# First stage of a two-block transformer kernel: two modulation blocks change engines, transfers are reordered, idle products are added on TensorE

## The reference

```python
c_act = jax.nn.silu(c)
mod = (c_act @ w_ada[l] + b_ada[l])[:, None, :]          # 1024 -> 6 * 1024
sh_m, sc_m, ga_m, sh_f, sc_f, ga_f = jnp.split(mod, 6, axis=-1)
h = _rms_norm(x, g_pre_mix[l]) * (1.0 + sc_m) + sh_m
y = _hybrid_mixer(h, ...)                                 # begins with h @ w_in
```

## Time and profile before

| what | value |
|---|---|
| median of 3 runs | 2115.19 us (2115.07 to 2115.41) |
| the profiled execution's own time | 2114.72 us |
| its span | 2112.9 us |
| TensorE busy | 2070.6 us, 98% |
| VectorE busy | 1385.5 us, 66% |
| ScalarE busy | 530.4 us, 25% |
| GpSimd busy | 806.1 us, 38% |
| VectorE's memsets of `ones` and `eps` (L480, L481) end | 0.99 us |
| VectorE's diagonal blocks of the norm (L493) end | 17.25 us |
| first product of the first half (L1029) | 26.64 us |
| first product of the second half (L1049) | 46.32 us |

### The profile page before, as it was taken

How to read it: one execution, slowest core, us unless ns; L and a number is a source line. 1 busy time by engine, 2 the same in 40 slices (tenths; PEclk the granted TensorE clock), 3 DMA queues, 4 the chain that set the end, 5 groups by cost and what they waited for, 6 DMA issues and landing times. The chain is left out here.

```text
span 2112.9 us, 25818 instructions
## 1 busy us (share of the span) xinstructions
PE 2070.6 (98%) x9793; PEld 1663.5 (79%) x9793; DVE 1385.5 (66%) x2297; ACT 530.4 (25%) x1256; POOL 806.1 (38%) x595
## 2 busy tenths in 40 slices
PE   8999999999999999999999999999999999999998
PEld 4446777777788888888888888888656888888887
DVE  7987956655343885376588886664626468888545
ACT  3443433333431000001401111113243431111101
POOL 0100200000104666656178887630011127787742
PEclk9999999999999999999999999999999999999999
DMA  9752555545322444453222323431132123232331
GB/s 379 242 185 76 157 182 178 156 129 143 113 80 80 160 160 160 135 168 110 86 80 80 120 68 106 126 120 50 43 123 80 50 92 99 80 113 62 82 84 40
DMA packets 244557, 252.27 MB, mean 119 GB/s; under 512 B 10010, under 2 KB 194772, under 8 KB 244180
## 3 DMA queue, kind: packets, MB, share of 16 engines
q1 hardware_dynamic: 243552, 249.17, 37.0%
q10 hardware_dynamic: 884, 1.46, 0.3%
HBM read 245.12 MB, written 4.21 MB: 118 GB/s over the span
## 5 line engine op out<-in xcount | busy, mean ns | idle before, releaser
L2809 POOL TENSOR_TENSOR w_sums<-ring 128x512 f32<-128x512 f32 x34 | 47.5, 1396 | 372.2 <-POOLq L1647 291.8
L2070 PE MATMUL ps<-h_act,ring 128*128 128x256 f32 x512 | 112.9, 379 | 0.9 <-PEq L1647 0.6
L2856 POOL TENSOR_TENSOR hidden<-rstd,h_act 128x256 f32<-128x256 f32 x34 | 32.2, 947 | 204.7 <-DVE h_act L3161 204.7
L2070 PEld LDWEIGHTS ps<-h_act,ring 128*128 128x128 f32 x512 | 96.8, 190 | 14.4 <-issue 1.5
L1049 PE MATMUL ps<-h_act,ring 128*128 128x512 f32 (+1 forms) x240 | 104.2, 593 | 0.0
L3161 DVE TENSOR_TENSOR h_act<-ps,rstd 128x256 f32<-128x256 f32 x46 | 19.5, 423 | 126.3 <-PE ps L2776 91.8
L2543 POOL TENSOR_TENSOR w_sums<-ring 128x256 f32<-128x256 f32 x96 | 89.8, 963 | 12.9 <-PE ps L2322 12.9
L2322 PE MATMUL ps<-pair_args,ring 128*128 128x256 f32 x384 | 90.7, 379 | 0.0
L2822 POOL TENSOR_TENSOR w_sums<-ring 128x768 f32<-128x768 f32 (+1 forms) x24 | 41.4, 1724 | 125.9 <-DMA ring<-in_ffn_w_out 84.0
L837 PE MATMUL ps<-h_act,ring 128*128 128x256 f32 x352 | 88.6, 394 | 0.7 <-ACT x_res L888 0.6
L849 PE MATMUL ps<-h_act,ring 128*128 128x256 f32 x352 | 88.5, 387 | 0.5 <-ACT rstd L896 0.5
(11 more groups left out here) (596 smaller groups left out, 5183.3 us busy)
## 6 DMA issues: line engine op xcount, KB each, us to landing
ring<-in_ffn_w_in SPq DMA_DIRECT2D x66, 1024.0 KB, 7.5
ring<-in_w_gate_up SPq DMA_DIRECT2D x22, 1024.0 KB, 7.8
ring<-in_ffn_w_out SPq DMA_DIRECT2D x32, 704.0 KB, 6.5
mod_half<-in_w_ada SPq DMA_DIRECT2D x16, 1024.0 KB, 8.7
ring<-in_w_mod SPq DMA_DIRECT2D x8, 2048.0 KB, 8.0
ring<-in_w_in SPq DMA_DIRECT2D x7, 2048.0 KB, 9.9
ring<-in_ffn_w_out SPq DMA_DIRECT2D x8, 1408.0 KB, 6.8
ring<-in_w_down SPq DMA_DIRECT2D x16, 704.0 KB, 6.6
```

The lines of the kernel that those rows point to most:

```text
L2070: ins = pe.matmul(K.ps[O.banks[i]][:, 0:b - a], w[:, k, (d % 4) * P:(d % 4) * P + P], K.h[:, k, CTX + a:CTX + b], start=(k == O.first(i)), ...
L2809: pool.tensor_tensor(s1, a21, a22, ALU.add).then_inc(S["wsum"].sem, 1)
L2856: pool.tensor_tensor(one[:, j], F.gate1[u % 2], F.got21[u % 2], ALU.mult)
```

## The change

Four things are done together.

1. Twenty-four idle products of 128 columns (`keep_running`, operands all ones, result unused) stand ahead of everything on TensorE; one and two more, of 512 columns, stand around `row_columns`.
2. Block 0 is now split: VectorE does k = 0 to 5 (`shift_sums`, six steps), TensorE k = 6 and 7 as a row. Block 2 is a row on TensorE, its first half of four products as soon as the first half of the transfer has landed; the spreading of the norm (`across`) stands in the middle of it. `shift_columns` adds the two parts of block 0: eight one-column products, four over 128 partitions, four over one.
3. SyncE's order: only half of the `dq` weights (k = 0 to 3) is loaded early, then the half blocks of blocks 1 and 3, then the context, then the rest of `dq`, then the constants.
4. The context is transposed two pieces at a time, two pairs between the last products of the first half and two behind it, and the waits for the context copies, the constants and the last normalised pieces stand further back on TensorE. On VectorE the normalising of k = 4 to 7 moves behind `half_sums`.

The semaphore `gates_in` becomes `parts_in` with counts that are 16 higher, and two counts in later stages follow; nothing else changes there.

```diff
+    def shift_sums():
+        w = K.ring.take(dve, ("ada", 0)).rearrange("p (k n) -> p k n", k=KT)
+        K.mods_summed += 2
+        acc = K.sq[:, 0, :]
+        for k in range(SHIFT_BY_DVE):          # 6
...
     dve.wait_ge(S.silu_done, 1)
-    sums_behind_row()
+    shift_sums()
     dve.wait_ge(S.across, 2)
...
-    for k in range(4, KT):
-        normalised(k)
     half_sums(2)
     half_sums(3)
+    for k in (4, 5):
+        normalised(k)
     coefficients(1)
+    for k in (6, 7):
+        normalised(k)
...
     act.wait_ge(S.across, 1)
-    act.activation(S.row, K.ps[7][0:1, :], ACT.Copy).then_inc(K.mod_sum, 1)
+    act.activation(S.row_shift, K.ps[1][0:1, :], ACT.Copy).then_inc(S.silu_done, 1)
+    act.wait_ge(S.across, 3)
+    act.activation(S.row, K.ps[0][0:1, :], ACT.Copy).then_inc(K.mod_sum, 2)
     start_scaled(K, S, act, 0)
...
 def start_tensor(K, S, pe):
+    pe.wait_ge(S.set_done, 1)
+    keep_running(K, pe, K.ps[7][:, 0:P], K.ones[:, :], 24)
     pe.wait_ge(S.ident_in, 16)
...
-    first_row(K, S, pe)
...
+    pe.wait_ge(S.par_done, 3)
+    first_rows(K, S, pe)
+    shift_columns(K, S, pe)
+    pe.wait_ge(S.kept, KT)
+    keep_running(K, pe, K.ps[1][:, :], K.x[:, 0, CTX:TOK], 1)
     row_columns(K, S, pe)
-    first_columns(K, pe, 2)
-    pe.wait_ge(S.par_done, 3)
-    pe.wait_ge(S.kept, KT)
+    keep_running(K, pe, K.ps[1][:, :], K.x[:, 0, CTX:TOK], 2)
...
+def first_rows(K, S, pe):
     w = K.ring.take(pe, ("ada", 0)).rearrange("p (k n) -> p k n", k=KT)
     pe.wait_ge(S.silu_done, 1)
+    for k in range(SHIFT_BY_DVE, KT):
+        last = pe.matmul(K.ps[1][0:1, :], K.cc1[:, k:k + 1], w[:, k, :], start=(k == SHIFT_BY_DVE), stop=(k == KT - 1))
+    last.then_inc(S.across, 1)
+    w = K.ring.take_begun(pe, ("ada", 2)).rearrange("p (k n) -> p k n", k=KT)
     for k in range(KT):
+        if k == 4:
+            across(K, S, pe)
+            K.ring.take(pe, ("ada", 2))
+        last = pe.matmul(K.ps[0][0:1, :], K.cc1[:, k:k + 1], w[:, k, :], start=(k == 0), stop=(k == KT - 1))
     last.then_inc(S.across, 1)
+def keep_running(K, pe, bank, rhs, n):
+    for _ in range(n):
+        pe.matmul(bank, K.ones[:, :], rhs, start=True, stop=True)
+def shift_columns(K, S, pe):
+    pe.wait_ge(K.dve.sem, SHIFT_BY_DVE)
+    pe.wait_ge(S.silu_done, 2)
+    for c in range(4):
+        pe.matmul(K.ps[7][:, c:c + 1], K.sq[:, 0, c * P:c * P + P], K.ones[:, 0:1], start=True, stop=False)
+        last = pe.matmul(K.ps[7][:, c:c + 1], S.row_shift[:, c * P:c * P + P], K.ones[0:1, 0:1], start=False, stop=True)
+    last.then_inc(K.mod_mm, 1)
...
-                    if (j, k) == (3, 2):
+                    if j == 3 and k in (1, 2):
+                        start_context(K, S, pe, k - 1)
+                    if (j, k) == (3, 3):
                         first_columns(K, pe, 3)
...
-            pe.wait_ge(S.ctx_kept, KT)
-            pe.wait_ge(S.const_in, 16)
-            pe.wait_ge(S.normed, KT)
+            start_context(K, S, pe, 2)
+            start_context(K, S, pe, 3)
```

More of the change, by code:

```diff
@@ L107 @@
 MODS_START = 4
+SHIFT_BY_DVE = 6
 MODS_FIRST = 6
@@ L283, in load_ahead @@
             name, parts = self.items[i]
-            for j, (dst, src) in enumerate(parts):
+            for j, (dst, src) in enumerate(parts[0:1] if name == "dq" else parts):
                 landed = self.begun[name] if j == 0 and name in self.begun else self.filled[i % RING]
@@ L554, in start_scalar, with context_turned @@
     act.wait_ge(S.across, 1)
-    act.activation(S.row, K.ps[7][0:1, :], ACT.Copy).then_inc(K.mod_sum, 1)
+    act.activation(S.row_shift, K.ps[1][0:1, :], ACT.Copy).then_inc(S.silu_done, 1)
+    act.wait_ge(S.across, 3)
+    act.activation(S.row, K.ps[0][0:1, :], ACT.Copy).then_inc(K.mod_sum, 2)
     start_scaled(K, S, act, 0)
-    for k in range(KT):
-        act.wait_ge(S.turned, KT + k + 1)
-        act.activation(K.x[:, k, 0:CTX], S.ctx_bank(k), ACT.Copy).then_inc(S.ctx_kept, 1)
+    context_turned(K, S, act, range(2))
+def context_turned(K, S, act, pairs):
+    for p in pairs:
+        act.wait_ge(S.turned, KT + p + 1)
+        act.activation(K.x[:, 2 * p:2 * p + 2, 0:CTX], S.ctx_bank(p).rearrange("p (a b) -> p a b", a=2),
+                       ACT.Copy).then_inc(S.ctx_kept, 1)
 def start_scaled(K, S, act, half):
@@ L589, in start_tensor, with start_context @@
         pe.transpose(K.ps[g - 1][:, 0:n], S.prow[0:n, g, :], const(K, "ident")[0:n, 0:n]).then_inc(S.par_t, 1)
-    first_row(K, S, pe)
[L591 to L595, removed]
-    row_columns(K, S, pe)
-    first_columns(K, pe, 2)
-    pe.wait_ge(S.par_done, 3)
-    pe.wait_ge(S.kept, KT)
-def start_context(K, S, pe, k):
-    if k == 0:
+    pe.wait_ge(S.par_done, 3)
[3 more added lines that the diff above has]
+    keep_running(K, pe, K.ps[1][:, :], K.x[:, 0, CTX:TOK], 1)
+    row_columns(K, S, pe)
+    keep_running(K, pe, K.ps[1][:, :], K.x[:, 0, CTX:TOK], 2)
+def start_context(K, S, pe, p):
+    if p == 0:
         pe.wait_ge(S.x_in[2], 16 * CC)
[L606 to L609, removed]
+    if p >= 2:
+        pe.wait_ge(S.ctx_kept, p - 1)
+    for i, (k, t) in enumerate(itertools.product((2 * p, 2 * p + 1), range(CC))):
+        last = pe.transpose(S.ctx_bank(p)[:, i * P:i * P + P], S.cr[t][:, k * P:k * P + P], const(K, "ident"))
     last.then_inc(S.turned, 1)
@@ L627, in start_sync @@
         sp.dma_start(S.half_buf[i][:, :, :], ada[:, 4 * half:4 * half + 4, 512 * n:512 * n + 512]).then_inc(S.half_in[i], 16)
+    for t in range(CC):
+        sp.dma_start(S.cr[t], c[:, t, :]).then_inc(S.x_in[2], 16)
+    K.ring.load_rest(sp, "dq")
     sp.dma_start(K.cst[:, P:NCONST], A["consts"][:, P:NCONST]).then_inc(S.const_in, 16)
@@ L1019, in _ @@
             start_tensor(K, S, pe)
-            w = K.ring.take(pe, "dq")
+            w = K.ring.take_begun(pe, "dq")
             for j in range(4):
```

79 lines of the change are left out of this document (39 added, 40 removed).

## The result

| kernel | median | runs | ratio to before |
|---|---|---|---|
| before | 2114.59 us (2112.20 to 2115.41) | 8 | |
| changed | 2120.52 us (2118.29 to 2121.34) | 8 | 1.0029 (1.0020 to 1.0038) |

The change costs 5.9 us. That is more than the 0.2% (4.2 us) that I had called no change, and above my range (up to 2119.8). The profiled execution took 2120.18 us with a span of 2118.4.

The account below looks back on a forecast made before the run. TensorE, busy 98% of the span, bounds the kernel. Block 2's row, added parts, idle products and columns put the first half at 31.1; plus 17.3, T moves +2.0: 2115.19 + 2.0, rounded to 2117.2 us, range 2114.8 to 2119.8.

Parts of the forecast that it names:

- first half: TensorE's stretch of products up to T: forecast to begin at 31.1 and take 17.3 us if the clock holds.
- adding block 0's parts: Eight one-column products of `shift_columns` on TensorE behind block 2's row, at 0.24 each: 1.94 us from 25.6.
- two idle products, wait for h: Between `row_columns` and the first half on TensorE: two idle products, 0.86 each, 1.72 us, where the wait took 1.40 before.
- T: Start of the second half's first product on TensorE: 46.32 before, forecast 48.3; its shift was to be the end's.
- The sum with the clock held: Main case: TensorE's clock does not fall ahead of T; T +2.0, time 2117.2 us, chance 0.57.
- first rival: Idle products don't hold the clock ahead of the first half: 1.7 us, T +3.7, 2118.9; 0.22 together with the second rival.
- A credit that never came: 2.4 us lost before between 26.64 and T, mostly to half clock; the forecast had this stretch without a gap.
- Behind T: After the second half's start: VectorE loses about 2.5 us, TensorE 2.0; VectorE has room, so nothing gained or lost.
- The second rival: Clock falls while TensorE waits for block 0 and parameters, 13.2 to 15.6: T +3.2, 2118.4; 0.22 together with first rival.
- The third rival: Clock falls both near 15 and between 25 and 31: +4.9, 2120.1; 0.10, including a fall together with a wait.
- The fourth: Rival: added work does not lie on the chain; T +0 or -0.3, time 2114.9 to 2115.2, chance 0.08.
- Faster by more than 0.2%: Whole kernel over 4.2 us faster: no mechanism, since the loss between 26.64 and T is 2.4 us; chance 0.03.

Follow-up runs that it names:

- a_again: The changed kernel profiled once more, unaltered, to see its clock; one execution, 2120.47 us.
- b_cols: b_order with eight more one-column products, results unused, ahead of `row_columns`; 2117.25 us, ratio 1.0013 to before.
- a_no_late: The changed kernel without its three idle products of 512 columns around `row_columns`; 2118.55 us, ratio 1.0019 to before.
- b_order: The kernel before with the change's transfer order, context pairs, VectorE order and later waits, but the old block division and no idle products; 2114.05 us, ratio 0.9999.
- b_early: The kernel before with only the 24 idle products at the start added; 2114.70 us, ratio 1.0004 to before.
- a_no_early: The changed kernel without the 24 idle products at the start; 2120.89 us, ratio 1.0032 to before.
- a_row: a_no_late with VectorE's part of block 0 summed by one row product in the middle of block 2's row; 2116.70 us, ratio 1.0013 to before.
- best1: b_order with the 24 idle products at the start and the filled gap of b_fill; 2112.36 us, ratio 0.9992 to before.
- b_order_fill: b_order with the filled gap of b_fill, without the 24 early idle products; 2112.27 us, ratio 0.9990 to before; repeated, 2111.92 us, 0.9989.
- b_fill: The kernel before with one 512-column and two 128-column idle products in the 1.40 us gap ahead of the first half; 2115.21 us, ratio 1.0004.
- a_mid: a_no_late with the eight one-column products of `shift_columns` moved to the middle of block 2's row; 2119.47 us, ratio 1.0023 to before.

## Why the prediction was wrong

The direction and the chain were right, the size was not. By its own steps, each against the profile after:

| step | forecast | measured | off by |
|---|---|---|---|
| block 2's row ends | 25.60 | 25.77 | +0.2 |
| adding block 0's parts | 1.94 | 2.48 | +0.5 |
| one idle product | 0.86 | 1.60 | +0.7 |
| `row_columns` | 0.97 | 1.80 | +0.8 |
| two idle products, wait for h | 1.72 | 3.57 | +1.9 |
| first half | 17.2 | 17.43 | +0.2 |
| T | 48.3 | 52.65 | +4.4 |

- **The step that failed** is "The sum with the clock held (+2.0, 2117.2): 0.57", and with it the first rival's price of 1.7 us for a fall. The sum has the idle products and `row_columns` at full clock (0.86, 0.97 and 1.72); they took 1.60, 1.80 and 3.57. The first half, where I had written "if the clock holds", took 17.43 for 17.2. The first rival's mechanism is what happened: one-column products and idle products did not hold the clock, a_again shows it a second time, and b_cols makes it out of the one-column products alone. Its price was mis-sized: I took the fall of before, 3.4 us, as the length of any fall. It was 6.8 us, which at half pace costs 3.4 and not 1.7. The four rows of the table from the idle product to the first half are 3.6 to 3.7 us over together, about that. With a price of 3.4 us the rival would have said T +5.4 and not +3.7, and with the 0.5 of the next point +5.9, beside the +6.3 measured.
- **A credit that never came**: the +2.0 of the forecast is what is left after 2.4 us, lost in before ahead of T, had been booked as won back. By the same prices the division of the blocks without idle products would cost 0.9 us of T (25.6 + 1.94 + 0.97 + 1.40 + 17.3 = 47.2). In a_no_late, where the clock fell, T is 3.1 later than in b_order.
- **A smaller miss**: 0.24 us for a one-column product came from rows in which all of one kind stand together (L710, L720). In `shift_columns` two kinds alternate, over 128 partitions and over one, and take 0.31 each (26.08 - 25.77). In b_cols most of them are 0.30 to 0.32 apart too.
- **Idle products on the chain**: the forecast had one of them as a plain cost and two as cover for the wait for h. At half clock the two are no cover but the delay: ScalarE begins on h at 32.15 and has the first piece near 33.0, TensorE comes to it at 35.22. Taking all three away gained 2.0 us of time (a_no_late).
- **The block division** was forecast as a cost of the change and is the larger part of it. b_order, without it and without idle products, is at 2114.05; a_no_late, which differs from it by the division and the early products, at 2118.55: 4.5 us, beside 2.0 for the three idle products.
- **The reorder** was costed at nothing and is nothing (b_order), and **the early idle products** too (b_early, a_no_early): the last one ended at 8.4 and not 8.9. Their pace rose near 5.0 and not near 5.5: the slices of 1 us up to there count 7 instructions and those behind it 11, where one that crosses an edge counts twice. The transposes behind them ran at 0.11 us each, as forecast (pairs 0.22 apart from 9.67 to 12.07).
- **Behind T** nothing was to be gained or lost. TensorE's waits up to 184 are the same, as forecast; the 0.8 us between T and the span comes from the later falls of the clock and the waits around them, which I had not looked at.
- **The second rival** did not happen in the changed kernel's profiles, but did in a_row's, in the place that I had named, with 3.4 us of low clock. Its wait of 1.75 us ahead of the rows stands in the changed kernel as well.
- **The third rival**, both falls, named 2120.1, close to the 2120.5 measured. That is chance: its fall near 15 did not happen, and the fall that did was twice as long as it assumed. **The fourth**, added work off the chain, did not happen: the first half began at 35.2 and not before 29.
- **Faster by more than 0.2%** had no mechanism in the rows. The best kernel found, some 2 us under before, agrees with that: I had counted 2.4 us as lost ahead of T, and no kernel of this study got back more than about that.

What stays open: why the same stretch falls in one execution and holds in another. best1 and b_order_fill have it alike ahead of the fill, and only best1's profile shows the fall. No run changes the moment of the one-column products without changing something else.

## What to carry to other kernels

A product that only keeps an engine running is free where the engine would have waited anyway, and counts at its full length, or at twice its length when the clock is down, where it stands ahead of something on the chain. The gap of 1.40 us that before had was such a place; the changed kernel closed the gap with work and put the idle products on top. And a time won on the engine that bounds the kernel is kept only if whatever it waits for next is early too: fill and reorder were each worth nothing alone and 2 us together.

## What the runs showed of the hardware

Up to T the low stretches of TensorE's clock came in two lengths only, over twelve profiles (the two of b_order_fill have none). It was 3.4 us in before, a_no_late, b_order, b_fill, best1 and a_row; 6.8 us in the changed kernel (twice), a_mid, b_cols, b_early and a_no_early. In the first group TensorE was in products of 512 columns as the clock fell, or within 0.3 us of it (a_no_late: fall at 30.5, first half at 30.76). In the second it was still in one-column products, or in nothing, or came back to such products (the changed kernel: one idle product, then 1.8 us of columns). Being busy by the profile was no protection: in a_no_early PE's busy share is 1.00 on both sides of the fall at 31.0, which came in the columns.

```profile
30.00:31.00 1.00, 1.00 (x6) 0.45 (x5) 0.00 (x0) 0.00 (x0) 0.00 (x0) 1.00 1.04 401
31.00:32.00 1.00, 1.00 (x7) 0.98 (x6) 0.00 (x0) 0.00 (x0) 0.00 (x0) 0.51 1.07 416
```

The same split shows in another stage, at the start of the attention, where TensorE waits 2.0 us. The line is from before:

```profile
273.62 0.80 PE L1657 MATMUL ps<-kv_t,q_t 64*128 64x128 f32 x4 [2.00 <-PEq L1249]
```

In three profiles the clock fell inside this wait, 0.5 to 0.8 us ahead of its end, and was low for 6.8 us (before from 272.9, a_no_late from 276.3, a_row from 275.2). In ten it fell after the wait, with TensorE in products again, and was low for 3.4 us. This is what the profiles show side by side; no run was made to test it, and why a stretch has the one length or the other stays open.
